# Third block of a transformer kernel: norm factors as columns, another order of heads and values, filter taps spread through the attention

## The reference, cut to what matters

```python
h = rmsnorm(x, g_mix)                       # x = rms_norm(h, final_norm) of block two
a_in, q, k, v, f_logit, gate_a, gate_b = split(h @ w_in)
a = a_in[:, :512] * sigmoid(a_in[:, 512:])
a = causal_depthwise_conv(a, w_dw, b_dw)    # 31 taps, 512 channels
y_conv = silu(layernorm(a)) @ w_conv_out
q, k = rmsnorm(q, g_q), rmsnorm(k, g_k)     # per head of 64
c = cumsum(log_sigmoid(f_logit + b_forget))
s = q @ k.T / 8 + c[q] - c[k]               # causal, 8 heads
y_attn = softmax(s) @ v @ w_attn_out
x = x + (sigmoid(gate_a) * y_conv + sigmoid(gate_b) * y_attn) @ w_out
x = x + feed_forward(rmsnorm(x, g_ffn))
```

## Time and profile before

| what | us |
|---|---|
| median of 3 runs (2266.36 to 2271.43) | 2267.72 |
| the profiled execution's own time | 2265.0 |
| its span | 2263.2 |
| TensorE busy | 2094.8 |
| VectorE busy | 1311.9 |
| ScalarE busy | 984.4 |
| GpSimd busy | 916.6 |

### The profile page before, as it was taken

The page is one execution under the profiler, slowest core; times in us unless marked ns, Lnnn a source line. Parts: engine busy times, 40 slices in busy tenths (PEclk is TensorE's granted clock), DMA queues, the critical chain, the costliest instruction groups (busy, mean ns, idle before and its releaser), DMA issues. The chain is left out here.

```text
span 2263.2 us, 28052 instructions
## 1 busy us (share of the span) xinstructions
PE 2094.8 (93%) x9602; PEld 1688.6 (75%) x9602; DVE 1311.9 (58%) x1853; ACT 984.4 (43%) x1550; POOL 916.6 (41%) x660
## 2 busy tenths in 40 slices
PE   6899899999999879899999999887887899999999
PEld 4677578788887667778788887765676678888887
DVE  6388856646264668866636264667869756213222
ACT  4577644434244456644434244434742244423222
POOL 4322034544445421134545445442114345545544
PEclk9999799999999989999999999998989999999999
DMA  3211022322222210013222222221102122322233
GB/s 140 76 55 47 19 72 87 102 93 102 93 93 93 75 56 29 29 56 103 93 94 101 94 101 93 74 84 56 38 19 75 56 84 93 102 95 101 93 101 104
DMA packets 49920, 179.61 MB, mean 79 GB/s; under 512 B 5536, under 2 KB 5664, under 8 KB 49824
## 3 DMA queue, kind: packets, MB, share of 16 engines
q1 hardware_dynamic: 48384, 174.09, 22.8%
q10 hardware_dynamic: 1440, 4.21, 0.5%
HBM read 176.18 MB, written 2.10 MB: 79 GB/s over the span
## 5 line engine op out<-in xcount | busy, mean ns | idle before, releaser
L472 POOL TENSOR_TENSOR wlo<-raw,whi 128x512 fp32r<-128x512 f32 x656 | 916.4, 1419 | 1332.2 <-ACT whi L926 1331.0
L480 PE MATMUL PS<-Bhi,whi 128*128 128x512 f32 x2368 | 944.2, 399 | 62.0 <-POOL wlo L472 30.8
L480 PE MATMUL PS<-Blo,whi 128*128 128x512 f32 x2368 | 930.2, 393 | 0.0
L480 PE MATMUL PS<-Bhi,wlo 128*128 128x512 f32 x2368 | 929.9, 393 | 0.0
L926 ACT ACTIVATE whi<-raw 128x1024 fp32r<-128x1024 f32 x328 | 345.5, 1056 | 580.6 <-PE PS L480 508.3
L480 PEld LDWEIGHTS PS<-Bhi,whi 128*128 128x128 f32 x2368 | 450.4, 190 | 180.9 <-issue 47.1
L480 PEld LDWEIGHTS PS<-Blo,whi 128*128 128x128 f32 x2368 | 451.0, 190 | 93.6 <-issue 2.2
L480 PEld LDWEIGHTS PS<-Bhi,wlo 128*128 128x128 f32 x2368 | 449.6, 190 | 95.2
L1399 DVE TENSOR_TENSOR AR<-PS,R 128x512 f32<-128x512 f32 x172 | 116.6, 689 | 219.7 <-PE PS L480 207.8
L1449 DVE TENSOR_TENSOR X<-X,PS 128x512 f32<-128x512 f32 x96 | 65.9, 687 | 235.2 <-PE PS L480 234.4
L1646 DVE SCALAR_TENSOR_TENSOR AR<-AR,par_sb 128x511 f32<-128x511 f32 x88 | 117.5, 1336 | 9.1 <-ACT AR L1148 9.1
(11 more groups left out here) (198 smaller groups left out, 2152.0 us busy)
## 6 DMA issues: line engine op xcount, KB each, us to landing
raw<-in_weights SPq DMA_DIRECT2D x328, 512.0 KB, 3.2
X<-in_xT ACTq DMA_DIRECT2D x4, 512.0 KB, 7.7
out<-X SPq DMA_DIRECT2D x8, 256.0 KB, 2.7
AR<-in_pT ACTq DMA_DIRECT2D x2, 512.0 KB, 4.5
con_sb<-in_constants ACTq DMA_DIRECT2D x1, 333.0 KB, 9.2
par_sb<-in_parameters ACTq DMA_DIRECT2D x1, 322.0 KB, 4.5
AR<-in_positions ACTq DMA_DIRECT2D x1, 256.0 KB, 9.3
AR<-in_lambdas ACTq DMA_DIRECT2D x1, 128.0 KB, 9.1
```

The source lines that it names most:

```text
L472: ins = pool.tensor_tensor(wlo[:, j, c], raw[:, j % RAWS, c], f32(whi[:, j, c]), ALU.subtract)
L480: return pe.matmul(out, w, x, start=start, stop=stop)
```

## The change

1. **Column norms.** `norm_sum` now makes four one-column matmuls, with a block of the summed squares as the stationary operand, so the sums of 128 tokens stand on 128 partitions, 4 columns in all. Root and reciprocal work on these. `spread_norm` brings the factor back to all partitions with four matmuls of 128 columns (the column broadcast as stationary operand, the identity moving), half a tile later, and VectorE copies it from PSUM to `R`. `row_to_column` and `columns` go. This holds for all nine norms.
2. **Both factors from one root.** ScalarE squares X times the final gain directly. From the two sums m (of x*x) and s (of (x*gain)^2), `mix_factors` forms both radicands, takes one root of 8 columns and one reciprocal. The products that make X (now `final_norm`) move behind the gates and the forget rows.
3. **Heads.** `head_sums` and the new `head_spread` do the same for the head norms, in 4 and 8 small matmuls. The 512-column reciprocal of each head tile goes; the product reads the factor in PSUM.
4. **Order.** TensorE: the forget gate's rows between a3 tiles 5 and 6, then head tiles 0 and 1 (a stage of their own, `qk3a`), then values with the sums and spreads between their slabs. The slabs' order follows.
5. **Taps.** 26 ahead of the attention, then 3, 3, 2, 1 in each four steps of it (36), 5 instead of 8 behind each gb3 tile, the other 22 behind ao3's products.
6. **Block one's attention.** The outputs' norm makes the usual division by the first softmax's sum unnecessary: VectorE no longer scales the first probabilities, and eps enters the sum of squares as eps times that sum squared, by four short matmuls for heads 0 to 5 and again for 6 and 7.

```diff
 def norm_sum(norm):
     pe.wait_ge(sq_used, KC * (NORMS.index(norm) + 1))
-    mm(PS[:, 7, :], ones, acc[:, :], True, True).then_inc(ss_done, 1)
+    src, c = (R, TB) if norm == "mix" else (acc, 0)
+    for t in range(TB):
+        last = mm(PS[:, 7, c + t:c + t + 1], src[:, t * P:t * P + P], one, True, True)
+    last.then_inc(ss_done, 1)
+def spread_norm(norm):
+    pe.wait_ge(rcol_ready, NORMS.index(norm) + 1)
+    ...
+    for t in range(TB):
+        last = mm(PS[:, 7, t * P:t * P + P], src[:, t:t + 1].broadcast_to((P, P)), ident, True, True)
+    last.then_inc(rspread, 1)
 # factor
-    dve.reciprocal(R[:, :], sq[:, 0, :]).then_inc(r_ready, 1)
+    dve.reciprocal(rcol[:, :], rootc[:, :]).then_inc(rcol_ready, 1)
+    dve.wait_ge(rspread, n + 1)
+    dve.tensor_copy(R[:, :], PS[:, 7, :]).then_inc(r_ready, 1)
 # TensorE, third block
-    tiles("a3", 4, hi, lo, KC, ready, "final", lead=3)
-    for t in range(4, 8):
-        tile("a3", 0, t, hi, lo, KC)
-        if t == 5:
-            norm_sum("mix")
-    row_to_column()
-    values("v3", "final", 4, T, range(4))
+    tiles("a3", 4, hi, lo, KC, ready, lead=3)
+    tile("a3", 0, 4, hi, lo, KC, halfway=mix_sums)          # norm_sum("final"), norm_sum("mix")
+    tile("a3", 0, 5, hi, lo, KC, halfway=lambda: spread_norm("mix"))
     ... # forget rows
+            if k == KC // 2 - 1:
+                spread_norm("final")
+    for t in range(6, 8):
+        tile("a3", 0, t, hi, lo, KC)
     for t in range(2):
-        project_qk("qk3", "final", t)
+        project_qk("qk3a", "final", t)
+    values("v3", "final", 4, T, (0,))
     head_sums(0)
-    project_qk("qk3", "final", 2)
     head_sums(1)
-    attention(3, "final", ((3, 0, 2), (3, 1, 2)))
+    values("v3", "final", 4, T, (1,))
+    head_spread(0)
+    head_spread(1)
+    values("v3", "final", 4, T, (2, 3))
+    project_qk("qk3", "final", 0)
+    attention(3, "final", ((1, 0, 2), (1, 1, 2)))
+def head_spread(t):
+    bank, _ = tile_of(*qk3(t))
+    pe.wait_ge(hinv_ready, t + 1)
+    for b in range(TB):
+        for s in range(2):
+            one_head = hinv[:, t % 2, 2 * b + s:2 * b + s + 1].broadcast_to((P, 64))
+            last = mm(PS[64 * s:64 * s + 64, bank, b * P:b * P + P], one_head, ident, True, True)
+    last.then_inc(hspread, 1)
 # VectorE, attention of block three, step g
+        if kind == 3 and g and halfway is not None:
+            head_inverse(halfway)
         if g + AHEAD[kind] < steps:
             maxima(kind, g + AHEAD[kind])
+        if kind == 3:
+            taps(TAPS_A_STEP[g % 4])                         # (3, 3, 2, 1)
 # VectorE, ahead of that attention
-    taps(22); values_low("v3", 1, T); taps(4); forget rows; head_scaled(0) ...
+    forget rows; final_norm(); zero_padding("v3"); taps(4); head_scaled(0) ...
+    head_scaled(1); taps(6); head_inverse(0), (1); taps(6); head_norm(0), (1) ...
+    taps(10); values_low("v3", 1, T); head_scaled(2); head_inverse(2)
 # VectorE, a3 tiles 2q + u: the last pair is taken 6, 7 instead of 7, 6
-    for u in (1, 0):
+    for u in (1, 0) if q < 3 else (0, 1):
```

More of the change, by code:

```diff
@@ L109 @@
 _c = 0
-for _name, _n in (("ident", P), ("before", P), ("after", P), ("ones", P), ("heads", P),
+for _name, _n in (("ident", P), ("before", P), ("after", P), ("ones", 1), ("heads", 2),
                   ("pick", 16), ("minus", 8), ("freq", 1), ("sign", 1)):
@@ L128, in constants @@
     put("ones", 1)
-    put("heads", i[:, None] // 64 == i[None, :] // 64)
+    put("heads", i[:, None] // 64 == np.arange(2)[None, :])
     put("pick", np.arange(16)[None, :] == 7)
@@ L255, in build @@
         ident = f32(identR)
-        ones = ccon("ones")
+        one = ccon("ones")
+        ones = one.broadcast_to((P, P))
         rC, rS = ar(0)[:, 0, :], ar(512)[:, 0, :]
@@ L542, in tiles @@
                 for j in range(lead, 4):
-                    tile(stage, 0, j, hi, lo, nk)
+                    tile(stage, 0, j, hi, lo, nk, halfway=(lambda: spread_norm(norm))
+                         if norm and j == lead else None)
                 if n > 8:
@@ L554, in split_of, with values @@
                 return chunks(Bhi[b]), chunks(Blo[b]), (x_split, KC * SPLITS.index(norm))
[L556 removed]
+            def values(stage, norm, slabs, width, parts, half=0, tell=True, halfway=None):
                 hi, lo, _ = split_of(norm)
@@ L573, in values @@
                             last = mm3(out, hi[:, k, tk], lo[:, k, tk], w, v, k == 0, k == KC - 1)
+                        if halfway and t == TB // 2 - 1:
+                            halfway()
                     if tell:
                         last.then_inc(slab_done, 1)
-            def row_to_column():
-                row_to_column.n += 1
-                pe.wait_ge(r_ready, row_to_column.norms[row_to_column.n - 1] + 1)
-                for t in range(TB):
-                    last = mm(PS[:, 7, t:t + 1], R[0:1, t * P:t * P + P], ones[0:1, 0:1], True, True)
-                last.then_inc(rcol_done, 1)
-            row_to_column.n = 0
-            row_to_column.norms = [NORMS.index(n) for n in ("attn0", "attn1", "mix")]
             def project_qk(stage, norm, t, part=0, parts=1):
@@ L756, in attention @@
                     project_qk(PROJ[kind], norm, t, part, parts)
+                    if kind == 3 and part == 0:
+                        head_sums(2)
                 if kind > 1:
@@ L765, in attention @@
                         scores(kind, g + AHEAD[kind])
+                    if kind == 3 and g and finished(kind, g - 2) is not None:
+                        head_spread(finished(kind, g - 2))
                     if piece(kind, g):
-                        project_qk(PROJ[kind], norm, *piece(kind, g))
+                        t, part, parts = piece(kind, g)
+                        project_qk(PROJ[kind], norm, t - 2 if kind == 3 else t, part, parts)
                     if kind == 1:
@@ L1324, in _ @@
                 head_high(t)
+            values("v3", 1, 4, T)
+            used(*qk3(2))
             head_square(2)
@@ L1704, in _ @@
             own.step(dve.memset(f32(cc[:, :]), 0.0))
+            own.step(dve.memset(epsq[:, :], 1.0))
             dve.memset(eps[:, :], EPS).then_inc(consts_ready, 1)
@@ L1916, in _ @@
             head_scaled(1)
+            taps(6)
+            for t in range(2):
+                head_inverse(t)
+            taps(6)
             for t in range(2):
```

228 lines of the change are left out of this document (139 added, 89 removed).

## The result

The changed kernel takes 2232.56 us (median of 4 runs, 2230.89 to 2235.24), the kernel before 2267.72 beside it: 35 us faster by these medians. One run of the kernel before, of 4517 us, was disturbed and is left out. 2235 was forecast, with a range of 2224 to 2252. The profiled execution took 2232.72 (span 2230.9).

The account below looks back on a forecast made before the run. TensorE was taken to bound the kernel, except behind the third attention (VectorE's taps) and at single waits for norms' reciprocals. +1 - 12 + 2.5 - 24 = -32.5 from 2265.0 gave 2232.5, plus 2.7: 2235 us, range 2224 to 2252.

Parts of the forecast that it names:

- Other blocks: All blocks but the third: column norms' extra passes against shorter waits, +1 us in sum, bounds -5 to +8.
- +2.7 for the feed-forward norms: Three feed-forward norms: no TensorE wait there, so each costs its 0.9 us of extra passes in full.
- the two embedding norms: Embedding norms: TensorE waits for VectorE's chain and R is 0.3 us later, +0.6 us.
- Up to the first projection: From 1457 us to the attention's first projection, third block: shorter waits and less slow clock, -12 us, bounds -18 to 0.
- the clock: Ahead of the attention's first projection: the loss from TensorE's lower level falls from 8.4 to 2.5 us.
- Attention: Third block's attention: steps 0 to 7 +6.5 by TensorE, the rest -4, together +2.5 us, bounds -6 to +33.
- rival 4: Attention: taps meet GpSimd's splits, 1.78 us each, +47 for that term, 2280 us in all; chance 0.04.
- Rival 3: Attention: taps lie on the path ahead of normalise and delay transposes, +33, 2266 us, no change; chance 0.08.
- the length of the attention (96 to 103): Sign that the forecast is right: the third block's attention lasts 96 to 103 us.
- Behind: From the attention's end to the last tap: 62 instead of 98 taps left, -24 us, bounds -29 (TensorE decides) to -18.
- 82 us of VectorE's work: Behind the attention: gb3 tiles 48, products 4.8, 22 taps 14.7, splits 9, start 5.9, against TensorE's 76.2.
- The sign of 80 to 85 us: Sign that the forecast is right: first to last tap behind the attention takes 80 to 85 us, VectorE nearly full.

Follow-up runs that it names:

- wide_ffn: Changed kernel with the norms ahead of three feed-forwards and two embedding gates done the old way (512-column sum, root, reciprocal, no spreading): 2228.62 us, ratio 0.9837.
- early_sigmoids: Changed kernel with ScalarE's gate sigmoids moved between its weight splits, three behind a3 tile 5's split, the fourth behind all: 2222.35 us, ratio 0.9803.
- spread_twice: Changed kernel with each of the eight head spreads done twice, the second writing the same values: 2231.29 us, ratio 0.9843.
- best: combo with 7 instead of 10 taps ahead of the values' low halves, 11 behind the third head's scaling, 28 in the attention: 2211.77 us, ratio 0.9763.
- combo: Changed kernel with sigmoids between splits, forget rows and X's products ahead of a3 tile 6, attention taps behind head-tile work: 2215.50 us, ratio 0.9773.
- after_no_taps: Changed kernel without taps in the attention, 8 instead of 5 behind each gb3 tile, the rest behind ao3's products: 2243.33 us, ratio 0.9888.
- taps_first8: Changed kernel with attention taps in steps 0 to 7 only, those of steps 8 to 15 moved behind it (7 per gb3 tile): 2236.84 us, ratio 0.9874.

## Why the prediction was right, and where only its sum was

**Other blocks: +1 forecast, -2.6 measured.** The term is not settled to its own size. In block two the wait of 3.71 us at 807.84 is gone, and the column is there early, as forecast (793.8). The -2.6 are a3's start 3.1 us earlier and a stretch behind the last tap 0.5 longer. The +2.7 for the feed-forward norms was too much: by wide_ffn two of the three cost 0.2 to 0.3 us, because a wait follows that takes the rest, and the third, with no wait behind it, the 1.0 in full; the two embedding norms came to 0.5 for 0.6. And a3's start is 1457.2 and 1458.3 in the two traces of kernels with the old norms, 1450.4 to 1461.0 (median 1453.8) in the eleven with all column norms; so some -3, with a scatter as large; what of it is block two's and what is block one's is open.

**Up to the first projection: -12 forecast, -10.0 measured.** The waits came as written: 7.00 us at bank 0 for 7.2, then 0.28 and 1.61 for 0.9, and 0.72 for the factor for 1.0. early_sigmoids shows the cause of the first: it hangs on the gates, and those on ScalarE's table load and sigmoids behind slab 7's split. The spreads were cheaper (1.09 for 1.8). The term that failed is the clock: I set 2.5 us for it. The granted clock is 0.93 over this stretch, 17.1 us at the lower level with TensorE busy in 14.7 of them, a loss of some 7, nearly the 8 of the kernel before. The idle time fell from 22.2 to 9.6 us, where 10.6 was forecast.

**Attention: +2.5 forecast, +8.1 measured.** This is the mis-sized term, and its parts were worse than its sum. I priced eight steps by TensorE's work (+6.5, the spreads) and let VectorE's 36 taps stand beside it. Measured: head norms -8.4, taps +16.5. A second set of spreads can't be seen in the time and added 3.2 us to the attention of one trace (spread_twice), so the +6.5 was too much for the first; the head norms gained 8.6 us in steps 8 to 15 (4.3 of idle time, and 4.3 less of busy time for 21 records more, at clock 0.92 for 0.79) and nothing in 0 to 7, where TensorE was already busy for 45 of 47.9 us. For VectorE I took away five reciprocals (16.8 us) in one place and six (20.1) in the sums of the two halves; six is right. The taps' own duration was right:
```profile
L1931 DVE SCALAR_TENSOR_TENSOR AR<-AR,par_sb 128x512 f32<-128x512 f32 x36 | 30.5, 892 | 0.0
```
0.89 us is the mean, as forecast (under 0.9; rival 4 needed 1.4). The Trainium skill, "SBUF — State Buffer", section "Who interferes with whom", says that a Vector instruction with two SBUF inputs contends with a GpSimd one that reads SBUF. That fits: GpSimd is busy for 11.5 of these 104.9 us, and behind the attention, where it is busy for 39.2 of 78.0, a tap takes 1.09 us in the mean. What I left out is what a tap does to TensorE's clock. With taps there are short waits, and stretches at the lower level, which were 11.5 of the 16.5 us; that the one brings the other is my reading of the traces, in which they come and go together. Rival 3 (taps on the path, +33) said that transposes would wait for over 20 us; they waited for 7.2, less than before, and idle time is only 5 us of what the taps cost. Of the signs that I had set, the length of the attention (96 to 103) was missed by 2 us, for this reason.

**Behind: -24 forecast, -27.7 measured.** The bound of TensorE's work (-29) nearly came, because VectorE took only 74.8 us and nothing was waited for but 0.2. My 82 us of VectorE's work was too much: I had charged more for the splits' collisions than they cost (60 of the 62 taps took 61.6 us, where my terms for all are some 67), and a start of 5.9 us, which stands beside TensorE's first tiles. The sign of 80 to 85 us for this stretch was missed too, at 77.3.

So the total of -32.5 (measured -32.3) is right by its two large terms, behind the attention and ahead of it, and by errors (measured less forecast) of -3.6, +2.0, +5.6 and -3.7 that cancel, which is luck. The step from the profiled execution to the median, +2.7, did not come again (2232.72 and 2232.56), and is the whole difference between 2235 and the measured time. The rest of the kernel, 473.4 for 472.9 us, did not change, as forecast.

## What to carry to other kernels

Work that is moved from a full engine into another's idle time is priced by two things: the waits that it makes, and the clock that TensorE loses beside them. Compare TensorE's busy time for the same number of records; if it grew, the clock did it. Before counting extra passes on TensorE, look for the next wait on the same chain: of 1.0 us of passes ahead of a wait 0.2 to 0.3 were left here, and with no wait behind them all of it. And where a wait stands in front of a bank, follow its releaser to the engine that holds a finished input (here sigmoids queued behind a weight split that had nothing to do with them); the order of a few lines was worth 7 us in the trace and 10 by the medians.

## What the runs showed of the hardware that I had not expected

- The code ahead of a3 is the same in eleven of these kernels, and TensorE reaches a3 at 1450.4 to 1461.0 us. By the starts of ScalarE's weight splits, best is 3.5 us behind combo at 314 and 4.7 from 350 to 675, 2.7 at 790 and 7.2 from 983 to block three: it moves across the attentions and the gates, where TensorE is not full, and stays constant through the feed-forwards. So in one trace a difference of under 5 us ahead of block three can't be put down to an edit.
- The stretch from a3 to the first projection is 117.8 us in the changed kernel, and 122.4 in two kernels with the same instructions there (after_no_taps and taps_first8). There the third head's square is waited for 5.1 us instead of 1.6, and the lower level follows. TensorE came to it only 0.4 us earlier, counted from a3; VectorE came to that head's scaling 3.1 us later. The wait for bank 0 had ended 1.0 us later, and from there on ten of VectorE's instructions take about 1.77 us beside GpSimd's splits, where the changed kernel has eight such; a tap alone takes 0.74. So a shift of one microsecond decides which instructions meet a split, and the stretch came out 4.6 us longer.
- Two float32 passes with 64 output columns each, on different sides, start 0.01 us apart; 16 of them take 1.09 us at full clock, and 1.98 at the lower level.
